# Expert gates of the first 128 tokens through a table in DRAM, in a two-block transformer kernel

## What is computed

```python
def peer_ffn(x, w_query, subkeys, u_tab, v_tab):
    ...
    sv, si = lax.top_k(s, PEER_TOPK)          # 8 heads, 2 halves of 128 keys, 16 best of each
    cand = (sv[..., 0, :, None] + sv[..., 1, None, :])          # 256 candidates
    ...
    top_s, pos = lax.top_k(cand, PEER_TOPK)   # 16 experts of 128 x 128, per token and head
    expert = jnp.take_along_axis(cand_id, pos, axis=-1)
    gate = jax.nn.softmax(top_s, axis=-1)
    ...
    act = gelu(einsum('thkd,td->thk', u_tab[expert], x))
    out = einsum('thk,thkd->td', gate * act, v_tab[expert])
```

## Time and profile before

| | us |
|---|---|
| median of 3 runs (1729.35 to 1730.93) | 1729.79 |
| the profiled execution | 1728.95 |
| its span | 1727.2 |

### The profile page before, as it was taken

How to read it: one execution, slowest core, us unless ns; L and a number is a source line. 1 busy time by engine, 2 the same in 40 slices (tenths; PEclk the granted TensorE clock), 3 DMA queues, 4 the chain that set the end, 5 groups by cost and what they waited for, 6 DMA issues and landing times.

```text
span 1727.2 us, 31786 instructions
## 1 busy us (share of the span) xinstructions
PE 1659.1 (96%) x10330; PEld 1414.0 (82%) x10330; DVE 1279.0 (74%) x2649; ACT 1015.0 (59%) x2026; POOL 72.4 (4%) x74
## 2 busy tenths in 40 slices
PE   7999999999999888999999999998999999999997
PEld 6867998888888766888888888877888889988886
DVE  5556569999996799788888775577766667676666
ACT  5445566666666798555555564346655545555553
POOL 0000000000000266000000000000000000000000
PEclk9999999999999999999999999999999999999999
DMA  6655555666666532788888664301466545556562
GB/s 245 217 204 177 157 157 187 192 187 190 191 187 193 183 124 97 273 289 291 310 288 289 215 194 130 110 25 37 135 187 190 183 153 152 179 164 189 187 184 96
DMA packets 87375, 316.98 MB, mean 184 GB/s; under 512 B 9841, under 2 KB 10113, under 8 KB 86785
## 3 DMA queue, kind: packets, MB, share of 16 engines
q1 hardware_dynamic: 85824, 310.35, 55.7%
q10 hardware_dynamic: 1184, 3.49, 0.6%
q0 software_dynamic: 288, 2.10, 0.3%
HBM read 314.85 MB, written 1.05 MB: 183 GB/s over the span
## 4 chain that ended last, share of the span: by engine, by line
PE 89%; DVE 5%; ACT 3%; issue 2%; DMA 1%; POOLq 0%; DVEq 0%; SPq 0%; ACTq 0%
PE acc L519 22%; PE bank L529 21%; PE acc L520 11%; PE bank L519 11%; PE bank L530 10%; PE bank L520 5%; PE bank L941 4%; ACT arena L1222 2%; PE acc L634 1%; DVE w_lo L1765 1%; DMA arena<-in_con 1%; DVE small L2329 1%; PE acc L673 0%; ACT L1222 0%; PE bank L666 0%
## 5 line engine op out<-in xcount | busy, mean ns | idle before, releaser
L1222 ACT ACTIVATE w_hi<-raw 128x512 fp32r<-128x512 f32 x982 | 613.2, 631 | 521.4 <-PE acc L519 249.9
L1765 DVE TENSOR_TENSOR w_lo<-raw,w_hi 128x512 fp32r<-128x512 f32 x982 | 663.3, 690 | 330.3 <-ACT w_hi L1222 328.6
L529 PE MATMUL bank<-x_both,w_hi 128*128 128x512 f32 x1532 | 536.7, 396 | 1.1 <-DVE x_both L2437 0.7
L530 PE MATMUL bank<-x_both,w_lo 128*128 128x256 f32 x1532 | 426.2, 278 | 0.0
L529 PEld LDWEIGHTS bank<-x_both,w_hi 128*128 128x128 f32 x1532 | 287.4, 188 | 71.2 <-issue 2.5
L530 PEld LDWEIGHTS bank<-x_both,w_lo 128*128 128x128 f32 x1532 | 288.0, 188 | 0.6
L519 PE MATMUL bank<-x_both,w_hi 128*128 128x256 f32 x1384 | 253.6, 285 | 10.1 <-DVE w_lo L1765 7.9
L519 PEld LDWEIGHTS bank<-x_both,w_hi 128*128 128x128 f32 x1384 | 216.3, 192 | 15.6 <-issue 8.0
L519 PE MATMUL acc<-w_hi,x_both 128*128 128x512 f32 x560 | 219.3, 392 | 4.1 <-DVE w_lo L1765 3.0
L519 PE MATMUL acc<-w_lo,x_both 128*128 128x512 f32 x560 | 218.6, 390 | 0.0
L520 PE MATMUL acc<-w_hi,x_both 128*128 128x512 f32 x560 | 218.6, 390 | 0.0
(11 more groups left out here) (272 smaller groups left out, 1819.2 us busy)
## 6 DMA issues: line engine op xcount, KB each, us to landing
raw<-in_peer_u SPq DMA_DIRECT2D x128, 512.0 KB, 3.5
raw<-in_peer_v SPq DMA_DIRECT2D x128, 512.0 KB, 4.4
raw<-in_mlp_w SPq DMA_DIRECT2D x128, 512.0 KB, 3.5
raw<-in_w_in SPq DMA_DIRECT2D x25, 512.0 KB, 5.0
route<-in_ada_w SPq DMA_DIRECT2D x24, 512.0 KB, 5.5
ada_x<-in_ada_w SPq DMA_DIRECT2D x24, 512.0 KB, 4.2
route<-in_ada_t SPq DMA_DIRECT2D x24, 512.0 KB, 4.7
ada_x<-in_ada_t SPq DMA_DIRECT2D x24, 512.0 KB, 4.8
```

The lines of the kernel that those rows point to most:

```text
L529: first = mm(ps[:, :], w[0], x_joined[:, :, c * T:(c + 1) * T], start=(c == 0), stop=False, **kw)
L530: return first, mm(ps[:, 0:T], w[1], x_hi[:, c * T:(c + 1) * T], start=False, stop=(c == KC - 1), **kw)
L1222: return nc.scalar.activation(dst, src, f, **kw)
L1765: v.tensor_tensor(w_lo[:, unit(n, half)], raw[:, a:a + HALF], w_hi[:, unit(n, half)].bitcast(F32), ALU.subtract).then_inc(s["lo_done"], 1)
```

## The change

The first 128 tokens no longer pass through the gate stage; it has 4 rounds of 8 groups instead of 8, with the same twelve half rows between them. Their gates go another way:

- POOL clears a table of 8 MB in DRAM in the u stage, with eight transfers of 1 MB, each waited for. The table has the layout of `arena`: 64 pairs of i, 128 j, 128 tokens, 2.
- DVE works out each gate's place in the table during the routing of `tt` = 0, and the gates themselves (`shares`) after tile 58; ACT takes their exponentials at the start of round 7.
- POOL sends them with 128 indirect transfers, one for each head and rank, each of 128 elements of 4 bytes (one a token), which add to the table. It waits for completion after every 16, the ranks of a head.
- SP waits for all 128, then reads the table back, 128 KB for each pair (1 KB a partition) into four slots, and in the v stage one more pair behind each second tile.
- POOL multiplies each pair's first 256 elements by it (`gate_pair`), 64 instructions of 128x256, and ACT's `gated_high` waits for that. POOL's 1 MB load stands behind pair 51.

```diff
+GATE_ROUNDS = P // 32
+SENT_ROUND = 7
+PAIRS = NKEYS // 2
+PAIR = 2 * P
+ZERO = 4 * D // 2
...
+        iT, jT, gT, njT = (small[:, k * (P + 16):(k + 1) * (P + 16)] for k in range(4))
+        pair_slots = [small[:, D + m * PAIR:D + (m + 1) * PAIR] for m in range(4)]
+        first_gate = nat[:, 2 * TT * P:(2 * TT + 1) * P]
+        first_place = nat[:, TT * P:(TT + 1) * P].bitcast(U32)
+        no_gates = arena[:, NKEYS * T - ZERO:]
+        g_dram = nc.dram_tensor("first_gates", (PAIRS * P * PAIR, 1), F32).ap()
+        g_pairs = g_dram[:, 0].rearrange("(n p f) -> n p f", p=P, f=PAIR)
...
+            def pair_gates(m, i):
+                sp.dma_start(pair_slots[m], g_pairs[i * 4 + m]).then_inc(pair_full[m], 16)
+
+            sp.wait_ge(s["gates_sent"], 16 * P)
+            sp.wait_ge(s["route_copied"], 2)
+            for m in range(4):
+                pair_gates(m, 0)
...
-            wait_freed(sp, "g", 7, 7 * 2)
+            wait_freed(sp, "g", 7, (GATE_ROUNDS - 1) * 2)
...
+            def next_pair(q, i=0):
+                if q % 2:
+                    sp.wait_ge(s["pair_gated"], i * 4 + (q // 2 + 1))
+                    pair_gates(q // 2, i + 1)
+
             for q in range(ROUND):
                 load("v", RAW + q, ins["peer_v"][RAW + q])
+                next_pair(q)
             with sp.Fori(1, ADA_DOT_ROUNDS) as i:
...
                 for q in range(ROUND):
                     load("v", RAW + q, ins["peer_v"][i * ROUND + (RAW + q)], i)
+                    next_pair(q, i)
...
+                    for m in range(2 - k):
+                        a = (4 * k + 2 * m + 1) * P
...
-                    if (8 * i + g - 3) * 2 * ADA_GATES // 61 >= halves_done and halves_done < 2 * ADA_GATES:
+                    if (8 * i + g - 3) * 2 * ADA_GATES // (8 * GATE_ROUNDS - 3) >= halves_done and halves_done < 2 * ADA_GATES:
...
+                    if sent and q == 0:
+                        act.wait_ge(s["zeroed"], 16 * (PAIRS * PAIR // ZERO))
+                        act.wait_ge(s["first_scores"], 1)
+                        fn(first_gate, first_gate, ACT.Exp).then_inc(s["gate_exp"], 1)
...
+            wait_freed(act, "g", 7, (GATE_ROUNDS - 1) * 2)
 
             def gated_high(q, i):
                 act.wait_ge(s["unit_started"], i * (2 * ROUND) + (2 * (TILE["v"][0] + q - 3) + 1))
+                act.wait_ge(s["pair_gated"], i * 4 + (q // 2 + 1))
                 fn(x_hi[:, q % 4 * T:(q % 4 + 1) * T], expert_pair(i, q // 2)[:, q % 2, :], ACT.Copy)\
                     .then_inc(s["gated_hi"], 1)
...
+            nc.gpsimd.memset(no_gates, 0.0).then_inc(s["zero_made"], 1)
+            wait_full(pool, "u", 0)
+            pool.wait_ge(s["zero_made"], 1)
+            rows_of_zeros = g_dram[:, 0].rearrange("(n p f) -> n p f", p=P, f=ZERO)
+            for n in range(PAIRS * PAIR // ZERO):
+                pool.dma_start(rows_of_zeros[n], no_gates).then_inc(s["zeroed"], 16)
+                pool.wait_ge(s["zeroed"], 16 * (n + 1))
+            pool.wait_ge(s["places_ready"], 1)
+            pool.wait_ge(s["first_gates"], 1)
+            for head in range(PEER_H):
+                for k in range(TOPK):
+                    n = head * TOPK + k
+                    nc.gpsimd.indirect_dma_start(g_dram, bass.IndirectOffsetOnAxis(first_place[:, n:n + 1], 0),
+                                                 first_gate[:, n:n + 1], None, compute_op=ALU.add).then_inc(s["gates_sent"], 16)
+                pool.wait_ge(s["gates_sent"], 16 * TOPK * (head + 1))
+
             pool.wait_ge(s["route_copied"], 2)
-            with pool.Fori(0, 8) as i:
+            with pool.Fori(0, GATE_ROUNDS) as i:
...
-            pool.wait_ge(s["v_full"], 7)
-            pool.dma_start(ctx_sb, ins["ctx"]).then_inc(s["in_ctx"], 16)
+            def gate_pair(m, i):
+
+                pool.wait_ge(pair_full[m], i * 16 + 16)
+                e = arena[:, bass.ds(i * (ROUND * T) + m * 2 * T, PAIR)]
+                nc.gpsimd.tensor_tensor(e, e, pair_slots[m], ALU.mult).then_inc(s["pair_gated"], 1)
+
+            pool.wait_ge(s["u_ready"], TILE["u"][1] // 2)
+            with pool.Fori(0, PAIRS // 4 - 4) as i:
+                for m in range(4):
+                    gate_pair(m, i)
+            for i in range(PAIRS // 4 - 4, PAIRS // 4):
+                for m in range(4):
+                    gate_pair(m, i)
+                if i == PAIRS // 4 - 4:
+                    pool.wait_ge(s["v_full"], 7)
+                    pool.dma_start(ctx_sb, ins["ctx"]).then_inc(s["in_ctx"], 16)
...
+            def shares(scores, exps_done):
+
+                gate = scores.rearrange("p (h k) -> p h k", k=TOPK)
+                total = gsum[:, 0:PEER_H]
+                dve.wait_ge(s["gate_exp"], exps_done)
+                then_wait(v.tensor_reduce(total, gate, AX, ALU.add))
+                then_wait(v.reciprocal(total, total))
+                return v.tensor_tensor(gate, gate, total.unsqueeze(2).to_broadcast([P, PEER_H, TOPK]), ALU.mult)
...
+                    if pace["next"] == SENT_ROUND * ROUND + 3:
+                        shares(first_gate, 1).then_inc(s["first_gates"], 1)
...
+                if tt == 0:
+                    odd = sif[:, hp:2 * hp]
+                    then_wait(v.tensor_scalar(odd.bitcast(U32), idx.bitcast(U32), 1, None, ALU.bitwise_and))
+                    then_wait(v.tensor_copy(odd, odd.bitcast(U32)))
+                    own = ids.rearrange("p (h s a) -> p s h a", h=PEER_H, s=2)[:, 0]
+                    then_wait(v.tensor_scalar(own, own, float(PAIR * P // 2), None, ALU.mult))
+                    step(v.scalar_tensor_tensor(own, odd.rearrange("p (h s a) -> p s h a", h=PEER_H, s=2)[:, 0],
+                                                float(1 - PAIR * P // 2), own, ALU.mult, ALU.add))
...
+                if tt == 0:
+                    assert pace["next"] <= SENT_ROUND * ROUND
+                    row = nat[:, 0:P]
+                    then_wait(v.scalar_tensor_tensor(row, nat[:, TT * P:(TT + 1) * P], float(PAIR), row, ALU.mult, ALU.add))
+                    v.tensor_scalar(first_place, row, C("twice"), None, ALU.add).then_inc(s["places_ready"], 1)
...
-            with dve.Fori(0, 8) as i:
+            with dve.Fori(0, GATE_ROUNDS) as i:
...
-                    e = experts[:, bass.ds(i * 32 + 4 * g, 4)]
+                    e = experts[:, bass.ds(i * 32 + (P + 4 * g), 4)]
```

More of the change, by code:

```diff
@@ L66 @@
                     ("conv_w", 3 * KC), ("conv_b", KC), ("ln_g", 4 * KC), ("ln_b", 4 * KC), ("lam", 4))
-CON, NCON = columns(("ident", P), ("mean_d", P), ("eps", 1), ("eps_small", 1), ("one", 1), ("mean_128", P), ("mean_64", P), ("zeros", P),
+CON, NCON = columns(("ident", P), ("mean_d", P), ("eps", 1), ("eps_small", 1), ("one", 1), ("twice", 1), ("mean_128", P), ("mean_64", P), ("zeros", P),
                     ("iota", P), ("head_mean", 3 * 32), ("sum_groups", ADA_COLS))
@@ L160, in build @@
         ada_full = [ctx.enter_context(nc.semaphore(f"ada_full{i}")) for i in range(ADA_RING)]
+        pair_full = [ctx.enter_context(nc.semaphore(f"pair_full{i}")) for i in range(4)]
         ada_x_full = [ctx.enter_context(nc.semaphore(f"ada_x_full{i}")) for i in range(ADA_BATCH)]
@@ L925, in _ @@
             halves_done = 0
-            for i in range(8):
+            for i in range(GATE_ROUNDS):
                 for g in range(8):
                     n = g // 4
-                    if (8 * i + g - 3) * 2 * ADA_GATES // 61 >= halves_done and halves_done < 2 * ADA_GATES:
+                    if (8 * i + g - 3) * 2 * ADA_GATES // (8 * GATE_ROUNDS - 3) >= halves_done and halves_done < 2 * ADA_GATES:
                         half_slab(halves_done // 2, 4 * (halves_done % 2))
@@ L1441, in gelu, with expert_round @@
                 fn(expert_pair(i, k), expert_pair(i, k), ACT.Gelu).then_inc(s["u_ready"], 1)
-            def expert_round(i, first=False, last=False):
+            def expert_round(i, first=False, last=False, sent=False):
                 for q in range(ROUND):
@@ L1485, in _ @@
             expert_round(0, first=True)
-            with act.Fori(1, rounds - 1) as i:
+            with act.Fori(1, SENT_ROUND) as i:
+                expert_round(i)
+            expert_round(SENT_ROUND, sent=True)
+            with act.Fori(SENT_ROUND + 1, rounds - 1) as i:
                 expert_round(i)
@@ L1492, in _ @@
             squares(1)
-            with act.Fori(0, 7) as i:
+            with act.Fori(0, GATE_ROUNDS - 1) as i:
                 for n in range(1, 1 + len(J_ACT)):
@@ L2112, in _ @@
                     next_tile(pace["next"] + q, i)
-            gate = nat[:, 2 * TT * P:3 * TT * P].rearrange("p (h k) -> p h k", k=TOPK)
             for q in range(ROUND):
@@ L2682, in constants @@
            "iota": np.tile(q, (P, 1)), "eps": np.full((P, 1), EPS), "eps_small": np.full((P, 1), EPS / 1024.0),
-           "one": np.ones((P, 1)), "sum_groups": (q[:, None] % ADA_COLS == np.arange(ADA_COLS)[None, :]),
```

(1 more changed line is left out.)

41 lines of the change are left out of this document (20 added, 21 removed), and 1 row of the table ADA_DOT_ROUNDS.

## The result

The changed kernel takes 1868.56 us (median of 4 runs, 1863.44 to 1872.98) against 1729.92 for the kernel before beside it: 1.0792 times as long, 95% interval 1.0774 to 1.0811. Forecast were 1685 us and a range of 1676 to 1740. What came true is the rival "sends slower than the gain".

A forecast was written before the change was run, and what follows sets the result against it. PE was taken to bound the u and v stages, with DVE, PE and ACT nearly full together in the gate stage. -45.4 + 0.5 + 0.5 = -44.4 us against 1728.95 gave 1684.6, as median 1685 us; range 1676 to 1740.

The forecast's parts named there:

- sends slower than the gain: Rival: POOL's send queue at 1.63 us a send or more makes the kernel slower, 1803 us at 2.2; chance 0.11.
- The sends: POOL's 128 sends from 396 us stay hidden before its work at 583.3: value 0, bounds 0 and +276 us.
- the prediction's bounds: POOL's 128 sends: low 0.72 us each plus eight waits of 2.9, 115 us; high 3.62 us each, 463 us.
- points of decision: Time from send to send on POOL: hidden up to 1.28 us, slower than the gain from 1.63 us on.
- The price of lateness: Gate stage and v loads queue behind the sends: a late send delays everything by what it is late.
- The estimate by the Trainium skill: POOL's sends: fixed cost about 2.0 us a transfer, 128 paid in turn, 256 us and about 1754 us.
- The gate stage: 32 groups instead of 64, DVE's 11.6 us wait staying: stage 57.0 us, saving 45.4 (33.9 to 51.3).
- Clearing the table: POOL's eight 1 MB transfers in the u stage, 237 to 298 us: costs nothing, at most 3 us.
- The second exponential: ACT in the u stage: 3 us with two table loads, on an engine with free time; put down as 0.5 us.
- sends block DVE: Rival: each send keeps DVE from two-input steps for 0.72 us, 84 us on PE, 1769 us; chance 0.08.
- The v stage: Added table reads and POOL's multiplications (0.52 us each) stay hidden: nothing, plus 0.5 us for the first four reads.
- v loads: Rival in the v stage: loads late beside the table reads, up to 21.5 us, 1685 to 1707 us; chance 0.08.

The follow-up runs named there:

- 512 bytes: The changed kernel with half the descriptor memory for POOL's transfers (512 instead of 1,024 bytes a partition): 1992.42 us, one execution.
- 64-send run: The changed kernel with only the first four heads' 64 sends (other four heads' gates left out) and 2,048 bytes of descriptor memory: 1687.26 us, ratio 0.9749.
- copy version: The 64-send run with the second exponential (ACT's, on the first 128 tokens' scores) replaced by a copy: 1683.49 us, ratio 0.9731.
- 2048 bytes: The changed kernel with twice the descriptor memory for POOL's transfers (2,048 instead of 1,024 bytes a partition): 1799.12 us, ratio 1.0391.
- half-filled sends: The changed kernel with only the first 64 tokens by the table, 128 sends of 64 elements, 2,048 bytes, 6 gate rounds: 1795.36 us, ratio 1.038.
- without the addition: The changed kernel with sends that write instead of adding, 1,024 bytes of descriptor memory as there: 1728.04 us, one execution.
- 16 sends: The changed kernel with only the first head's 16 sends, the other seven heads' gates left out: 1687.02 us, ratio 0.9751.
- full sends of 64 tokens: The changed kernel with 64 tokens by the table, two gates a partition, 64 sends of 128 elements, 6 gate rounds: 1713.2 us (2,048 bytes), 1737.99 us (1,024).

## Why the prediction was wrong, step by step

- **The sends, the step that failed.** The measured 2.93 us a send lie between the prediction's bounds, 0.72 with the eight waits beside them at the low end and 3.62 at the high one. The low bound itself was out of reach: two sends never stood less than 1.84 us apart, which is over 1.63. The points of decision were sound: hidden up to 1.28 us, slower than the gain from 1.63. What was wrong was the value, put at nothing. "I take below that" rested on two reasons. One was that the program waits only once in 16; the machine paused after one to three sends for room in a memory that the prediction didn't look at, although its size stands in the kernel: 112 us. The other was that 1,024 elements had landed in 2.9 us, so the DMA engines couldn't set the pace. They were indeed far from busy (a share of 0.16 where sends run alone), but POOL set it, with 1.54 us to issue an adding transfer, where the nearest row, a direct load, had 0.72. Without a single pause and without the eight waits the change would still have been late: 236 us against 187.
- **The price of lateness** was right. POOL's first multiplication came 774.7 - 583.3 = 191.4 us later than before, and the first gating, with what had been prepared by then, 187.0. The prediction's sum with the latter gives 1684.6 + 187.0 = 1871.6, of which the gate stage gave back 50.1 - 45.4 = 4.7 more than forecast: 1866.9. 1867.4 were measured in the profiled execution.
- **The estimate by the Trainium skill** (DMA: Bandwidth & Descriptors, Anatomy of one DMA — SWDGE (gpsimd) path: about 2.0 us fixed a transfer, most of it completion) was nearer than the forecast, 1754 us, and for half the reason. The pauses of 1.8 to 2.1 us where nothing else runs are of that size; the 1.54 us of issuing come on top. The Trainium skill (Perfetto Trace Analysis, DMA Instruction — SWDGE (GPSIMD)) says that such an instruction's interval ends when its descriptors are written and not when the data have moved; by that reading 1.54 us is POOL's own work, and the trace agrees: with 512 bytes a send landed 3.0 us after its issue, 1.5 us after its interval had ended.
- **The gate stage** was forecast at -45.4 us, with DVE's wait of 11.6 us staying, and each gating at 1.70 to 1.80 us. In the 64-send run the gatings go from 596.8 to 650.5, 53.7 us against 100.9: -47.2, at 1.73 us each, with 9.5 us of waiting for PE. In the changed kernel it was -50.1, 1.64 us and 6.7. The wait of 11.6 us neither stayed nor halved in the 64-send run, and it was lower still after the long stop.
- **Clearing the table** cost nothing in the changed kernel: the last of 8 transfers was issued at 289 us, the DMA served 325 GB/s from 260 to 300 us, and PE was busy 40.00 of 40 us with 232 products, where before had 233. In six other runs PE's pace fell between 280 and 300 us (last section); whether the clearing has a part in that is open.
- **The second exponential** costs 1.2 us of PE's time, not 0.5, as the copy version shows. ACT had the free time, but its two table loads stand ahead of the rounding of a tile, and DVE and PE wait for that.
- **DVE and the sends.** The rival "sends block DVE" is refuted: its subtractions of 128x512 from 420 to 560 us have a median of 693 ns beside the sends and 692 in the same stretch of before, and with 48 more sends TensorE's products stayed at 794.
- **The v stage** is hidden as forecast. Stretch of the v stage in the changed kernel, against rows 4:

```profile
964.00:996.00 32.00, 32.00 (x143) 26.50 (x142) 28.48 (x49) 18.57 (x36) 8.23 (x6) 1.00 0.91 311
```

PE is full at 311 GB/s (forecast 315), so v loads aren't late. POOL's multiplication took 1.17 us in the mean, not the 0.52 of the forecast, and DVE's busy time rose by 2.5 us in 32 (26.0 to 28.5), within the 2.2 to 4.5 named for it, out of 6.0 free.

So the chances were wrong rather than the list of cases: 0.11 for the case that came, 0.57 for the one that needed t below 1.28 us, when no row of the trace had such a transfer and the two bounds were a factor of five apart.

## What to carry to other kernels

Before hiding a train of small transfers behind other work, price one of them on the engine that issues it, with its kind (direct, indirect, adding), and count how many of them the memory for descriptors holds: here a train of 64 with 2048 bytes went for nothing, and one of 128 with 1024 bytes held up the next stage by 187 us. Where a term's bounds lie a factor of five apart and the decision lies between them, weigh the cost of being wrong at each end and don't take the more pleasant one. And fill each transfer: the same gates took 275 us in 128 half-filled sends and 170 in 64 full ones, 1795 against 1713 us for the kernel.

## What the runs showed of the hardware

- An indirect adding transfer of 128 elements of 4 bytes into DRAM occupies POOL for 1.54 us, one of 64 elements 1.41, a writing one of 128 elements 0.96 (medians). In the u stage single ones of the changed kernel took up to 2.58 us, behind it (from 600 us on) none over 1.56. The next begins 0.30 us later where there is no pause. A direct load of 1 MB occupied it for 0.72.
- The pauses are 1.8 to 2.1 us where nothing else runs (changed kernel, from 606 us on). Beside the loads of u they are longer, 2.1 to 4.6 us, and one at 594 us, beside the loads for the gate and v stages, took 5.3. Idle times before two sends of the changed kernel:

```profile
424.81 2.00 POOL L1769 DMA_INDIRECT first_gates<-small  x1 [3.62 <-issue]
...
433.38 1.99 POOL L1769 DMA_INDIRECT first_gates<-small  x1 [4.60 <-issue]
```

  Later completion goes with it: with 512 bytes the median landing is 4.4 us in the u stage and 3.0 behind it. That the loads delay it is argued, since DVE, ACT and PE stop in the same moment and no run took the loads alone away.
- TensorE's pace in the u stage has two values while it is busy 20.00 of 20 us at a granted clock of 1.00: about 117 products in 20 us, or about 115. The kernel before kept 117 in both executions traced, and so did the changed kernel, but for the gap at 400 us. Six runs fell to 115 between 280 and 300 us: 2048 bytes, 512 bytes, without the addition, 16 sends, 64 sends of the copy version, and the half-filled sends, whose clearing had only four transfers, the last issued at 256 us. The 64-send run and the two with full sends of 64 tokens fell to it at the gap at 400 us. Two came back to 117 at that gap, 512 bytes and without the addition; the others stayed. Over 190 to 300 us the slower pace is 3 to 5 us, the rest of the longer u stage. In it the single products are longer, by 1.3%. From 440 to 540 us, before and the 16-send run:

```profile
L529 PE MATMUL bank<-x_both,w_hi 128*128 128x512 f32 x290 | 100.6, 394 | 0.0
L556 PE MATMUL bank<-x_both,w_hi 128*128 128x512 f32 x285 | 100.7, 399 | 0.0
```

  What switches it is open.
